# Row factors of three norms applied to the products, and five norms worked under other units, in a two-block transformer kernel

## What is computed

```python
def _rmsnorm(x, g):                       # eps 1e-5 here, 1e-6 in the second block
    y = x * lax.rsqrt(jnp.mean(x * x, axis=-1, keepdims=True) + NORM_EPS)
    return y * g

def first_block(...):                     # 16 + 512 tokens of 1024 features
    proj = _rmsnorm(h, g_mix) @ w_in      # z, xbc, dt, u
    y_ssd = _ssd_mixer(...)               # ends in _rmsnorm(y, g_norm)
    y_s5 = _s5_mixer(...)                 # ends in _rmsnorm(glu(y), g_norm)
    h = h + concatenate([y_ssd, y_s5]) @ w_out
    m = _rmsnorm(h, g_mlp) @ w_up
    h = h + square(relu(m)) @ w_down      # 4096 wide
    return _rmsnorm(h, g_final)[:, N_META:]

def second_block(...):                    # two layers; xc: 256 context tokens
    for l in range(2):
        h  = rmsnorm(x,  norm1_g[l]) * (1 + sc1)  + sh1
        hc = rmsnorm(xc, norm1_g[l]) * (1 + csc1) + csh1
        p = h @ w_in[l]                   # the context: all of it in layer 0, keys and values in 1
        x = x + g1 * gated_merge(p[..., QKV_END:], y_conv, y_attn, w_out[l])
        h2 = rmsnorm(x, norm2_g[l]) * (1 + sc2) + sh2
        x = x + g2 * conv_ffn(h2, w_up[l], ...)
        # in layer 0 the same for xc
    return rmsnorm(x, final_norm_g)
```

## Time and profile before

| what | value |
|---|---|
| median of 3 runs | 3190.62 us (3188.3 to 3192.59) |
| the profiled execution | 3188.98 us, its span 3187.2 us |
| busy: PE, PE weight loads, DVE, ACT, POOL | 2890.1 (91%), 2334.6 (73%), 1614.3 (51%), 1088.4 (34%), 1265.3 (40%) us |
| chain that ended last, by engine | PE 75%, DVE 12%, DVE's queue 4%, ACT 3%, DMA 2% |
| moved | 306.75 MB, 96 GB/s |

### The profile page before, as it was taken

The page is one execution under the profiler, slowest core; times in us unless marked ns, Lnnn a source line. Parts: engine busy times, 40 slices in busy tenths (PEclk is TensorE's granted clock), DMA queues, the critical chain, the costliest instruction groups (busy, mean ns, idle before and its releaser), DMA issues.

```text
span 3187.2 us, 41978 instructions
## 1 busy us (share of the span) xinstructions
PE 2890.1 (91%) x15576; PEld 2334.6 (73%) x15576; DVE 1614.3 (51%) x2057; ACT 1088.4 (34%) x1593; POOL 1265.3 (40%) x689
## 2 busy tenths in 40 slices
PE   6999877999999798898988999999978988899997
PEld 6975635777887687666767888888766667677786
DVE  6864773353333353388855422313246976552424
ACT  4534222332323131334433522313242453253423
POOL 3442200424444181387732323222337673434443
...
GB/s 173 94 97 213 165 254 190 106 53 106 97 94 79 93 125 107 126 89 70 60 66 66 66 51 68 66 60 60 73 67 106 73 56 58 99 74 91 98 88 71
DMA packets 116014, 306.75 MB, mean 96 GB/s; under 512 B 36128, under 2 KB 44448, under 8 KB 115232
## 3 DMA queue, kind: packets, MB, share of 16 engines
...
## 4 chain that ended last, share of the span: by engine, by line
PE 75%; DVE 12%; DVEq 4%; ACT 3%; DMA 2%; issue 2%; SPq 1%; ACTq 1%
PE ps L284 36%; PE ps L314 18%; PE ps L305 6%; DVE co L1960 3%; PE ps L1679 2%; PE ps L2069 2%; DVEq L1961 2%; PE ps L636 1%; DMA wraw<-w_ada 1%; DVE sm L1936 1%; DMA wraw<-stream 1%; DVE mv L2142 1%; PE ps L1683 1%; DVE nacc L412 1%; SPq L1204 1%
## 5 line engine op out<-in xcount | busy, mean ns | idle before, releaser
L245 POOL TENSOR_TENSOR wlo<-wraw,whi 128x1024 fp32r<-128x1024 f32 x373 | 924.0, 2487 | 1729.4 <-ACT whi L237 1728.2
L237 ACT ACTIVATE whi<-wraw 128x1024 fp32r<-128x1024 f32 x373 | 393.2, 1056 | 593.3 <-PE ps L314 189.6
L284 PE MATMUL ps<-xhi,whi 128*128 128x512 f32 (+2 forms) x1328 | 466.1, 369 | 1.7 <-issue 1.7
L284 PE MATMUL ps<-xlo,whi 128*128 128x512 f32 (+2 forms) x1328 | 465.3, 368 | 0.0
L284 PE MATMUL ps<-xhi,wlo 128*128 128x512 f32 (+2 forms) x1328 | 330.6, 368 | 0.0
L284 PEld LDWEIGHTS ps<-xhi,whi 128*128 128x128 f32 x1328 | 240.7, 188 | 46.3 <-issue 2.5
L284 PEld LDWEIGHTS ps<-xlo,whi 128*128 128x128 f32 x1328 | 240.5, 188 | 44.1
L284 PEld LDWEIGHTS ps<-xhi,wlo 128*128 128x128 f32 x1328 | 230.3, 188 | 43.5
L1960 DVE SCALAR_TENSOR_TENSOR co<-ub,vec,co 128x512 f32<-128x512 f32 (+1 forms) x216 | 252.2, 1207 | 5.0
L996 DVE SCALAR_TENSOR_TENSOR res<-ps,mod,res 128x512 f32 (+1 forms) x64 | 48.0, 750 | 281.1 <-PE ps L305 151.6
L2055 POOL TENSOR_TENSOR co<-co,ct 128x512 f32<-128x512 f32 (+1 forms) x144 | 163.9, 1138 | 20.8 <-issue 0.4
...
## 6 DMA issues: line engine op xcount, KB each, us to landing
wraw<-stream SPq DMA_DIRECT2D x425, 512.0 KB, 3.5
...
```

The lines of the kernel that those rows point to most:

```text
L237: act.activation(whi[:, s], wraw[:, s], ACT.Copy).then_inc(hi_done[s], 1)
L245: pool.tensor_tensor(wlo[:, s], wraw[:, s], whi[:, s].bitcast(F32), ALU.subtract).then_inc(lo_done[s], 1)
L284: last = pe.matmul(ps[:, bank, 0:b - a], w[:, s, kt], x[:, kt, c0 + a:c0 + b], start=start, stop=stop)
```

## The change

It has two parts.

1. **ssd, s5 and MLP norms.** The halves are made of the unscaled tiles (`raw_hi_act`: ACT Copy times the gain; `raw_lo_dve`), so the product does not wait for the row factor. The sums go into the quad (`between`), the rows behind it, DVE copies the row to `nrs` and multiplies the product by it when it evicts: in OUT1 and OUT2 by an extra in-place multiplication in `add_unit_dve` (`r=`), in the MLP's up units by one operation max(.,0) x r that takes Relu's place. The square of the MLP moves from DVE to ACT, ahead of the high half, and a unit's `split_hi` now stands after both. For ssd all 64 one-column sums stand inside OUT1's quad, and OUT1's second four weight units are loaded earlier.
2. **Five later norms.** c0's first norm (c0a) is worked under the MLP's last chunk; its sums stand between up units and down quad. The first block's final norm is summed in c0's first quad and applied in place in c0's mixing stage. l0's first norm (l0a) is squared in c0's merge, summed at its end, scaled under c0's out units; l0 then begins with four single units. c0b is worked under l0's out units, and three of the four first context products stand between l0's out units and the row of l0b. l1's first norm (l1a) is worked under c1's keys and values.

The order of the norms' numbers changes with this, and so do some buffers' places. POOL's list of operations stays the same.

The diff, cut to what the steps of the prediction speak of:

```diff
+            if between:
+                between()
...
+    def raw_hi_act(act, n, kt, src, g, dst):
+        act.activation(dst[:, kt, 0:SEQ], src(kt), ACT.Copy, scale=g(kt)).then_inc(n_hi.sem, 1)
+    def raw_row_dve(dve, n):
+        r = norm_row_dve(dve, n, SEQ)
+        dve.tensor_copy(nrs[:, 0:SEQ], r)
+        dve.drain()
+        return nrs[:, 0:SEQ]
+    def raw_lo_dve(dve, n, kt, src, g, hi, lo):
+        dve.wait_ge(n_hi.sem, n_hi.past("hi", hi_before[n] + kt))
+        dve.scalar_tensor_tensor(lo[:, kt, 0:SEQ], src(kt), g(kt), hi[:, kt, 0:SEQ].bitcast(F32), ALU.mult, ALU.subtract).then_inc(n_lo.sem, 1)
...
-    NORM = {"mix": 0, "ssd": 1, "s5": 2, "mlp": 3, "final1": 4, "c0a": 5, "l0a": 6, "l0b": 7, "c0b": 8,
...
+    NORM = {"mix": 0, "ssd": 1, "s5": 2, "mlp": 3, "c0a": 4, "final1": 5, "l0a": 6, "c0b": 7, "l0b": 8,
...
-        pe.wait_ge(d_wm.sem, d_wm.past("wm", 2 * (NCH - 2)))
-        for c in (1, 2):
-            ssd_sums_pe(pe, c)
         for g in range(2):
             ssd_y_pe(pe, NCH - 1, g)
         ada_turn(pe, 2)
-        for c in (NCH - 2, NCH - 1):
-            ssd_sums_pe(pe, c)
...
+            dve.tensor_tensor(ps[:, s, 0:T], ps[:, s, 0:T], r, ALU.mult)
+            dve.drain()
...
+    def out2_act(act):
+        n = NORM["mlp"]
+        added = lambda e, kt: e.wait_ge(acc_free[(U_OUT2 + kt) % R], read_out(U_OUT2 + kt))
+        for m in range(NT):
+            split_hi(act, U_OUT2 + m + R)
+            if m:
+                norm_square(act, n, m - 1, rsrc, SEQ, added)
+        s, rnd = slot(U_OUT2 + NT - 1)
+        act.wait_ge(unit_done[s], rnd + 2)
+        for kt in range(NT):
+            added(act, kt)
+            raw_hi_act(act, n, kt, rsrc, g1("g_mlp"), xhi)
+        norm_square(act, n, NT - 1, rsrc, SEQ, added)
+        norm_root_act(act, n, SEQ, "eps5")
+    def out2_dve(dve):
+        n = NORM["mlp"]
+        r = raw_row_dve(dve, NORM["s5"])
+        for m in range(NT):
+            add_unit_dve(dve, U_OUT2 + m, 0, 0, m, res, SEQ, r=r)
+            if m:
+                norm_add(dve, n, m - 1, SEQ)
+        dve.drain()
+        for kt in range(NT):
+            raw_lo_dve(dve, n, kt, rsrc, g1("g_mlp"), xhi, xlo)
+        norm_add(dve, n, NT - 1, SEQ)
+        norm_rec_dve(dve, n, SEQ)
+    def raw_pe(pe, U, n, xh, xl, sums):
+        pe_quad(pe, U, 0, 0, xh, xl, SEQ, between=sums, **normed(n))
+        norm_rows_pe(pe, NORM[n], SEQ)
+        for j in range(R):
+            pe_unit(pe, U + R + j, 0, 0, xh, xl, SEQ)
...
     def mlp_pe(pe):
-        def chunk(c):
-            pe_quad(pe, U_FF, c, 4, xhi, xlo, SEQ, **normed("mlp"))
+        n = NORM["mlp"]
+        def chunk(c, b, last=False):
+            pe_quad(pe, U_FF + 16 * b, c, 4, xhi, xlo, SEQ, between=None if b else lambda: norm_sums_pe(pe, n, SEQ), **normed("mlp"))
+            if not b:
+                norm_rows_pe(pe, n, SEQ)
             for j in range(4):
-                pe_unit(pe, U_FF + 4 + j, c, 4, xhi, xlo, SEQ)
-            pe_quad(pe, U_FF + 8, c, 4, hhi, hlo, SEQ, hi=lambda pe, kt: pe.wait_ge(m_h.sem, m_h.past("hi", c * 8 + kt)),
-                    lo=lambda pe, kt: pe.wait_ge(m_l.sem, m_l.past("lo", c * 8 + kt)))
+                pe_unit(pe, U_FF + 16 * b + 4 + j, c, 4, xhi, xlo, SEQ)
+            if last:
+                norm_sums_pe(pe, NORM["c0a"], CTX)
+            pe_quad(pe, U_FF + 16 * b + 8, c, 4, hhi, hlo, SEQ, hi=lambda pe, kt: pe.wait_ge(m_h.sem, m_h.past("hi", c * 8 + (8 * b + kt))),
+                    lo=lambda pe, kt: pe.wait_ge(m_l.sem, m_l.past("lo", c * 8 + (8 * b + kt))))
+            if last:
+                norm_rows_pe(pe, NORM["c0a"], CTX)
             for j in range(4):
-                pe_unit(pe, U_FF + 12 + j, c, 4, hhi, hlo, SEQ)
-        loop(pe, 4, chunk)
-    def mlp_act(act):
-        act.wait_ge(n_hi.sem, n_hi.past("hi", hi_before[NORM["mlp"]] + NT - 1))
+                pe_unit(pe, U_FF + 16 * b + 12 + j, c, 4, hhi, hlo, SEQ)
+        chunk(0, 0)
+        loop(pe, LAST - 1, lambda i: chunk(i, 1))
+        chunk(0, LAST, True)
...
-                s, rnd = slot(U_FF + m, c, 4)
-                act.wait_ge(unit_done[s], rnd + 2)
-                act.wait_ge(m_v.sem, m_v.past("v", c * 8 + m, 2))
-                ins = act.activation(rl[:, m % 2], ps[:, s, :], ACT.Relu)
-                ins.then_inc(acc_free[s], 1)
+                act.wait_ge(acc_free[(U_FF + m) % R], read_out(U_FF + m, c, 4))
+                act.wait_ge(m_l.sem, m_l.past("lo", c * 8 + m, 2))
+                act.activation(rv[:, m % 2], rl[:, m % 2], ACT.Square).then_inc(m_v.sem, 1)
+                act.wait_ge(m_v.sem, m_v.past("v", c * 8 + m))
+                act.activation(hhi[:, m], rv[:, m % 2], ACT.Copy).then_inc(m_h.sem, 1)
                 split_hi(act, U_FF + m + R, c, 4)
-                act.wait_ge(m_v.sem, m_v.past("v", c * 8 + m))
-                act.activation(hhi[:, m], rv[:, m % 2], ACT.Copy).then_inc(m_h.sem, 1)
+                if c is LAST:
+                    norm_square(act, first, m, context.src, CTX, lambda e, kt: e.wait_ge(s_c, 16))
...
+        norm_root_act(act, first, CTX, "eps6")
+        for m in range(R):
+            split_hi(act, N_B1 - 8 + m + R)
+        for kt in range(NT):
+            norm_hi_act(act, first, kt, CTX, context.modv(0), one=True)
+        for m in range(NT):
+            norm_square(act, NORM["final1"], m, lambda kt: res[:, kt], SEQ,
+                        lambda e, kt: e.wait_ge(acc_free[(N_B1 - 8 + kt) % R], read_out(N_B1 - 8 + kt)))
...
+                dve.scalar_tensor_tensor(rl[:, m % 2], ps[:, s, :], 0.0, r, ALU.max, ALU.mult).then_inc(acc_free[s], 1)
...
+        norm_rec_dve(dve, first, CTX)
+        for m in range(R):
+            add_unit_dve(dve, N_B1 - 8 + m, 0, 0, m, res, SEQ)
+        norm_scale_dve(dve, first, context.src, CTX, context.gain(0), context.modv(0), one=True)
+        for m in range(R, NT):
+            add_unit_dve(dve, N_B1 - 8 + m, 0, 0, m, res, SEQ)
+            norm_add(dve, NORM["final1"], m - R, SEQ)
+        for m in range(R, NT):
+            norm_add(dve, NORM["final1"], m, SEQ)
...
+        pe_quad(pe, p.U, 0, 0, xkhi, xklo, p.T, **normed(p.key + "a"))
+        norm_sums_pe(pe, then.norm(0), then.T)
         for j in range(4):
-            g = p.U + 4 + j
-            pe_unit(pe, g, 0, 0, xhi, xlo, p.T)
...
+        if p.one:
+            pe_quad(pe, p.U, 0, 0, xh, xlo, p.T, between=lambda: norm_sums_pe(pe, NORM["final1"], SEQ), **normed(p.key + "a"))
+            norm_rows_pe(pe, NORM["final1"], SEQ)
+        elif p.l == 0:
+            normed(p.key + "a")["hi"](pe, NT - 1)
+            normed(p.key + "a")["lo"](pe, NT - 1)
+            for j in range(R):
+                pe_unit(pe, p.U + j, 0, 0, xh, xlo, p.T)
+        else:
+            pe_quad(pe, p.U, 0, 0, xh, xlo, p.T, **normed(p.key + "a"))
...
+            norm_in_place_dve(dve, NORM["final1"], rsrc, SEQ, g1("g_final"))
...
+            norm_sums_pe(pe, NORM["l0a"], SEQ)
...
+        pe_quad(pe, p.U + 44, 0, 0, mhi, mlo, p.T, hi=lambda pe, kt: pe.wait_ge(p.m_h.sem, p.m_h.past("hi", kt)),
+                lo=lambda pe, kt: pe.wait_ge(p.m_v.sem, p.m_v.past("lo", kt)))
+        norm_sums_pe(pe, q.norm(1), q.T)
         for j in range(R):
+            pe_unit(pe, p.U + 48 + j, 0, 0, mhi, mlo, p.T)
+            if j == 0:
+                norm_rows_pe(pe, q.norm(1), q.T)
+        U = p.U + 52
+        first_context_pe(pe, U, q, 0)
+        first_context_pe(pe, U, q, 1)
+        norm_sums_pe(pe, p.norm(1), p.T, 7)
+        first_context_pe(pe, U, q, 2)
+        norm_rows_pe(pe, p.norm(1), p.T)
...
+        n = then.norm(0)
+        norm_root_act(act, n, then.T, "eps6")
+        for kt in range(NT):
+            norm_hi_act(act, n, kt, then.T, then.modv(0))
+        for m in range(R, NT):
             split_hi(act, p.U + 44 + m + R)
...
+        add = lambda m: add_unit_dve(dve, p.U + 44 + m, 0, 0, m, p.res, p.T, p.modv(2))
+        for m in range(R):
+            add(m)
+        norm_scale_dve(dve, n, then.src, then.T, then.gain(0), then.modv(0), also=lambda kt: add(R + kt // 2) if kt % 2 else None)
...
+            segment(U_OUT1 + R, U_OUT1 + R, R)
             sp.wait_ge(s_kept, 16)
             sp.wait_ge(n_lo.sem, n_lo.past("lo", 2 * NT - 1))
+            sp.wait_ge(d_sq.sem, d_sq.past("sq", NCH - 2))
             sp.dma_start(ks[:, :], pd).then_inc(s_back, 16)
             sp.dma_start(cc5[:, :], A["s5_bc"][:, 2:4]).then_inc(s_5c, 16)
...
-            norm_rows_pe(pe, NORM["ssd"], SEQ)
-            add_pe(pe, U_OUT1, 2, hhi, hlo, SEQ, **normed("ssd"))
+            raw_pe(pe, U_OUT1, "ssd", hhi, hlo, lambda: raw_sums_ssd(pe))
...
-            norm_pe(pe, NORM["s5"], SEQ)
-            add_pe(pe, U_OUT2, 2, xhi, xlo, SEQ, **normed("s5"))
-            norm_pe(pe, NORM["mlp"], SEQ)
+            raw_pe(pe, U_OUT2, "s5", xhi, xlo, lambda: norm_sums_pe(pe, NORM["s5"], SEQ))
             mlp_pe(pe)
```

(34 more changed lines are left out.)

361 lines of the change are left out of this document (212 added, 149 removed).

## The result

The changed kernel takes 3160.56 us, the median of 4 runs (3156.24 to 3164.35), against 3189.46 of the kernel before on the same chip: a ratio of 0.9902, 95% interval 0.9886 to 0.9918. (Ratios are estimated from the runs and are not quotients of two medians, which would be 0.9909 here.) By the medians 29 us are won, by the two profiled executions 24.6, where I forecast 47 (3144, range 3118 to 3168). The sign and the range held; a third of the gain is missing by the medians, nearly half by the traces, and the traces show where.

The account below looks back on a forecast made before the run. TensorE is busy 91% of the span, so only waits and slow clock can be won. 1+7.2+5.6-9.3-8.7+20.4+15.4+2.5+12.9 = 47.0 us off 3188.98, plus 1.6 for the median: 3144, range 3118 to 3168.

Parts of the forecast that it names:

- B: The s5 norm, at OUT2: pause and slow quad cost 15.4 us, 8.2 remain afterwards, 7.2 won.
- D: First block's final norm and c0's first norm: 16.4 us instead of 36.8 to c0's second four units, 20.4 won.
- E: l0's first norm, scaled under c0's out units: 15.4 us won.
- rival 2: DVE's moved work delays TensorE under c0: price 14 us, time 3158; chance 0.24 together with rival 4.
- A: The ssd norm, at OUT1: quad starts at 306.5, s5 stage at 368.6 instead of 369.60; 1 us won, -2 to +6.
- C: The MLP norm, at its first up quad: 14.8 us today, 9.2 remain afterwards, 5.6 won.
- C': What the MLP pays: 9.3 us lost at three up-to-down turns, 8.7 lost in the last chunk.
- F: Norms l0b and c0b: quad begins at 1743.8, quad and context sets end at 1768.7; 2.5 us won, -1 to +6.
- G: l1's first norm, under c1's keys and values: quad begins about 2351.4, 11.3 us earlier; 12.9 won.
- Rival 3: Clock falls at each new short pause and stays low for a quad; half a quad each gives 3208; chance 0.03.
- Rival 1: Clock hardly falls at the new pauses, so 18.9 us priced for it are saved: some 3125; chance 0.23.
- Rival 4: Row-factor evictions serialize after the rows, handing back B and C (13 us): 3157; chance 0.24 together with rival 2.

Follow-up runs that it names:

- e5: Changed kernel with the ssd norm worked as before the change, earlier weight loads kept: 3156.37 us, ratio 0.9887 to the kernel before.
- e4: Changed kernel with each group of eight one-column matmuls of the ssd norm's sums issued twice: 3167.63 us, ratio 0.9932 to the kernel before.
- e2: As e1, and in the MLP's first three chunks the weight split stands ahead of square and high half on ACT: 3135.4 us.
- e1: Changed kernel with the context's square ahead of the weight split on ACT in the MLP's last chunk: 3142.98 us.
- e6: Changed kernel with the three early context products of l0's FFN in slot order 1, 2, 0 instead of 0, 1, 2: 3154.7 us.
- e7: Changed kernel with c1's last values eviction on ACT ahead of high halves 4 to 7 of l1's first norm: 3157.13 us.

## Why the prediction was right in direction and short in size

- **B, D and E: right, within 1.1 us each.** In B the wait for the last `s5o` was 1.67 (2.0 forecast) and the stall behind the row 2.41 (2.3). Sums in the quad, rows behind it and scaling under other units hide the pause; c0's second four units begin 15.8 us after the MLP's end (16.4 forecast), with .23 of waiting for weights left of 1.14. The in-place scaling under c0's convolution cost nothing: from those units to the units at 1202.20 and 1200.97 both kernels take 110.0 us. So rival 2 is out.
- **A: right, as nothing,** as far as the scatter lets one see (e5); e4 shows that the s5 stage hides no sums. My 306.5 for the quad lies amid the starts found.
- **C failed** at the step "stall 1.5, since one operation replaces two". By the trace it is 4.2, as the fifth unit waits for a weight split queued behind square and high half on ACT. I had seen that order and priced it at the turns alone. e2 shows it: 1.94 with the split first. That is 2.7 of the 6.2 missing. The waits for the first high and low half came nearly as forecast, 2.34 and 1.49 (2.4 and 1.1). The largest miss is the last term, "clock 2.4": without its wait and sums the quad took 25.3 us (676.66 to 704.26 less 1.49 and .81), 3.9 over 21.39, and the four units behind it 23.69, 1.6 over the 22.13 of before (719.07 there), so 5.5 in all, 3.1 more than forecast. The granted clock was 0.85 and 0.94 there. No experiment varied this term.
- **C', the turns: right in kind.** The wait was 2.35 (2.46 forecast). The slow quad came behind it in two turns of three (22.96 and 22.97, but 21.36 at the second), so that 7.4 were lost, not 9.3. The granted clock over these quads was 0.93, 1.00 and 0.93. In e1 the slow quad came once in three.
- **C', the last chunk, failed** at "they want its last add, behind the last low half and a POOL split on DVE". The mechanism was right, and I charged it once, 7.2 us. It holds in every one of the eight steps, since each step's next eviction stands in the same queue. The steps begin only in the quad's tail, where four products come ready within some 5 us, and at 5.64 a step against TensorE's 5.53 a unit they never catch up. The wait was 17.97; e1 takes it to 3.42. The slower quad behind it (23.90, 2.5 over 21.39) was as forecast.
- **F failed** at "slot 0's weight split until about 1728.2". The wait was 7.18 and I had about 3.5, as I took slot 0's split to be done sooner; it is the fourth of four. e6 shows it. F's out quad was 1.4 slower besides (24.43 against 23.07).
- **G failed** at "the quad begins about 2351.4". I let the low halves' hold set the start; what set it was an eviction on ACT behind the high halves that they delay. That made the quad 5.4 us later than forecast, counted from c1's start, and it took 24.73 where my clock term left 23.6. e7 shows the first.
- **The rule weighed.** Between multiplication and addition with a drain written between them, 0.77 us lie from start to start (650.35 and 651.12 in the changed kernel's timeline), .07 more than the first takes. The .42 that I worked out from the Trainium skill, "VectorE: DVE Perf Modes", section "The DRAIN you can't avoid", do not show there. They do not show behind the row's copy either: at 649.59, with the same drain behind it, it takes .69 and the next operation starts at 650.35, .07 later. At 705.35 there are .37 until the next one, at 706.41; there a loop's start and two semaphore waits stand between, so that gap does not speak for the rule. It decided nothing.
- **The rivals.** Rival 3 (a low clock for a whole quad behind every short pause) is out: waits of 2.35 were followed by hot quads too, and the slow ones lost 1.6. Rival 1 was true at one turn of three and false in C. Rival 4's sign came in C, a wait of 4.20 behind the row, and C handed back all that I forecast for it; B did not.
- **Where luck helped.** The measured 3160.56 lies nearest the numbers of rivals 4 and 2 (3157 and 3158), by other mechanisms than theirs. The range, made for them, took in four misses that it had not been made for.
